# Turned blocks multiplied by the norm's weights once per PSUM bank, two low halves on GpSimd at two boundaries, and the orders around them laid anew

## The reference

```
def first_block(x, ...):            # mixer: RG-LRU branch + attention over 64 chosen keys
    h = rmsnorm(x, norm_mix_pre) @ w_in
    ...                             # rnn and attention, gated, then w_o
    x = x + rmsnorm(mix, norm_mix_post)
    h = rmsnorm(x, norm_ffn_pre)                 # boundary "f0"
    x = x + rmsnorm(swiglu(h), norm_ffn_post)
def second_block(x, ...):           # two layers
    for l in range(2):
        x = x + 0.5 * swiglu(rmsnorm(x, ffn1_norm[l]), ...)   # "f1", "f3"
        x = x + mixer_l(x)                                    # "ev" or "od"
        x = x + 0.5 * swiglu(rmsnorm(x, ffn2_norm[l]), ...)   # "f2", "f4"
```

## Time and profile before

| | us |
|---|---|
| median of 3 runs | 1407.73 (1406.33 to 1409.03) |
| profiled execution, own time | 1409.42 |
| its span | 1407.6 |
| PE busy | 1385.2 (98%) |
| DVE busy | 967.2 (69%) |
| ACT busy | 810.4 (58%) |
| POOL busy | 53.5 (4%) |

### The profile page before, as it was taken

The page is one execution under the profiler, slowest core; times in us unless marked ns, Lnnn a source line. Parts: engine busy times, 40 slices in busy tenths (PEclk is TensorE's granted clock), DMA queues, the critical chain, the costliest instruction groups (busy, mean ns, idle before and its releaser), DMA issues.

```text
span 1407.6 us, 19523 instructions
## 1 busy us (share of the span) xinstructions
PE 1385.2 (98%) x7290; PEld 1175.5 (84%) x7290; DVE 967.2 (69%) x1472; ACT 810.4 (58%) x1264; POOL 53.5 (4%) x62
## 2 busy tenths in 40 slices
PE   8999999999999999999999999999999999999999
PEld 7898788788887888888788888888888877888887
DVE  7999856667755676756977777556675584667753
ACT  6679944565645555545866555445554576565541
POOL 2021000000000000000000000000000070000000
PEclk9999999999999999999999999999999999999999
DMA  9544455476555566566346665566655541366651
GB/s 314 173 121 135 153 162 182 133 224 182 191 186 173 177 185 185 189 187 198 110 164 197 185 188 190 185 192 182 181 193 181 160 150 31 121 208 186 190 193 60
DMA packets 127213, 242.64 MB, mean 172 GB/s; under 512 B 7568, under 2 KB 13328, under 8 KB 127120
## 3 DMA queue, kind: packets, MB, share of 16 engines
q1 hardware_dynamic: 126208, 239.15, 55.0%
q0 software_dynamic: 624, 2.10, 0.5%
q10 hardware_dynamic: 288, 0.14, 0.0%
HBM read 240.31 MB, written 1.05 MB: 171 GB/s over the span
## 4 chain that ended last, share of the span: by engine, by line
PE 93%; DVE 4%; ACT 2%; issue 1%; DMA 0%; ACTq 0%; DVEq 0%
PE PX L347 24%; PE PX L361 16%; PE PX L363 16%; PE PX L362 16%; PE PX L349 12%; PE PX L407 3%; PE PX L652 2%; DVE WL L328 1%; PE PX L541 1%; PE PX L355 1%; PE PX L356 1%; PE PX L357 1%; PE PX L545 0%; ACT WH L322 0%; PE PX L1055 0%
## 5 line engine op out<-in xcount | busy, mean ns | idle before, releaser
L328 DVE TENSOR_TENSOR WL<-RAW,WH 128x1024 fp32r<-128x1024 f32 (+2 forms) x454 | 554.7, 1227 | 356.2 <-ACT WH L322 354.0
L322 ACT ACTIVATE WH<-RAW 128x1024 fp32r<-128x1024 f32 (+2 forms) x454 | 477.1, 1054 | 507.6 <-PE PX L363 268.1
L347 PE MATMUL PX<-AT,WH 128*128 128x512 f32 x1440 | 508.1, 398 | 0.0
L349 PE MATMUL PX<-AT,WL 128*128 128x256 f32 x1440 | 403.3, 280 | 0.0
L347 PEld LDWEIGHTS PX<-AT,WH 128*128 128x128 f32 x1440 | 270.5, 188 | 65.9
L349 PEld LDWEIGHTS PX<-AT,WL 128*128 128x128 f32 x1440 | 271.7, 189 | 0.2
L361 PE MATMUL PX<-WH,AT 128*128 128x512 f32 (+4 forms) x528 | 210.7, 399 | 6.4 <-DVE AT L1312 6.0
L363 PE MATMUL PX<-WH,AT 128*128 128x512 f32 (+4 forms) x528 | 201.9, 382 | 0.0
L362 PE MATMUL PX<-WL,AT 128*128 128x512 f32 (+4 forms) x528 | 201.4, 381 | 0.0
L361 PE MATMUL PX<-WH,FTh 128*128 128x512 f32 x440 | 171.6, 390 | 0.0
L363 PE MATMUL PX<-WH,FTl 128*128 128x512 f32 x440 | 171.3, 389 | 0.0
(11 more groups left out here) (333 smaller groups left out, 1327.9 us busy)
## 6 DMA issues: line engine op xcount, KB each, us to landing
RAW<-in_ffn_w_gu_dram SPq DMA_DIRECT2D x132, 512.0 KB, 3.7
RAW<-in_ffn_w_gu_2b_dram SPq DMA_DIRECT2D x88, 512.0 KB, 3.7
RAW<-in_w_in_dram SPq DMA_DIRECT2D x44, 512.0 KB, 3.7
RAW<-in_ffn_w_down_dram SPq DMA_DIRECT2D x44, 512.0 KB, 3.3
RAW<-in_ffn_w_down_2b_dram SPq DMA_DIRECT2D x44, 512.0 KB, 3.3
RAW<-in_w_ffn_down_dram SPq DMA_DIRECT2D x22, 512.0 KB, 3.6
RAW<-in_ev_w_in_dram SPq DMA_DIRECT2D x20, 512.0 KB, 3.6
RAW<-in_w_rnn_out_dram SPq DMA_DIRECT2D x8, 512.0 KB, 3.7
```

The source lines that it names most:

```text
L322: e.activation(WH[i % NHL][:, 0:m], RAW[i % NRAW][:, 0:m], ACT.Copy).then_inc(*up("hi", i))
L328: e.tensor_tensor(WL[i % NHL][:, 0:m], RAW[i % NRAW][:, 0:m], WH[i % NHL][:, 0:m].bitcast(F32), ALU.subtract).then_inc(*up("lo", i))
L347: e.matmul(PB[bank].rearrange("p (h s) -> p h s", h=2), h[:, f], AT0B[:, :, kx, :], start=start, stop=False, skip_group_check=True)
L349: ins = e.matmul(PB[bank][:, 0:S], l[:, f], p.src[0][:, kx, :], start=False, stop=stop, skip_group_check=True)
```

## The change

A new function `dve_block_gain` multiplies a whole bank by the norm's weights in one instruction, with the weights broadcast along the tokens, into a new SBUF tile XG; `act_block_hi` and `dve_block_lo` become one instruction each, from XG. At f0 and f1 the `lo` of the third and of the fourth chunk (chunks 76, 77 and 142, 143) runs on GpSimd, with a semaphore of its own, which `mm` and the loads into RAW wait for. The orders of PE, ACT, DVE and POOL in the start, the first mixer and at the four boundaries are laid anew. Nothing else is computed, and SP's order is the same.

```
+        POOL_LOW = [F[f][0][0].first + x for f in (0, 1) for x in (2, 3)]
...
+        def low(e, i):
+            m = stream[i][2] * stream[i][4]
+            e.wait_ge(*on("hi", i))
+            e.tensor_tensor(WL[i % NHL][:, 0:m], RAW[i % NRAW][:, 0:m], WH[i % NHL][:, 0:m].bitcast(F32),
+                            ALU.subtract).then_inc(*up(LOW(i), i))
...
+        def pool_lo(e, f, x):
+            low(e, F[f][0][0].first + x)
...
+        def dve_block_gain(e, n, b, c):
+
+            i = COLS[GAIN[n][0]] + GAIN[n][1] + 4 * c
+            e.wait_ge(*on("b_T", (n, b, c)))
+            e.tensor_tensor(block_room(b, c), PB[4 + 2 * b + c].rearrange("p (t s) -> p t s", t=4),
+                            CO[:, i:i + 4].unsqueeze(2).broadcast_to([128, 4, 128]), ALU.mult).then_inc(*up("b_g", (n, b, c)))
...
-            for i in range(4):
-                t = 4 * c + i
-                ins = e.activation(AT0[0][:, t, b * 128:b * 128 + 128], bank[:, i * 128:i * 128 + 128], ACT.Copy,
-                                   scale=gain(n, t))
-            ins.then_inc(*up("b_hi", (n, b, c)))
+            e.wait_ge(*on("b_g", (n, b, c)))
+            e.activation(AT0[0][:, 4 * c:4 * c + 4, b * 128:b * 128 + 128], block_room(b, c),
+                         ACT.Copy).then_inc(*up("b_hi", (n, b, c)))
...
+            e.tensor_tensor(AT0[1][:, 4 * c:4 * c + 4, b * 128:b * 128 + 128], block_room(b, c), hi_,
+                            ALU.subtract).then_inc(*up("b_lo", (n, b, c)))
```

More of the change, by code:

```diff
@@ L322, in hi, with LOW @@
                 e.activation(WH[i % NHL][:, 0:m], RAW[i % NRAW][:, 0:m], ACT.Copy).then_inc(*up("hi", i))
-        def lo(e, i):
[L325 to L329, removed]
+        POOL_LOW = [F[f][0][0].first + x for f in (0, 1) for x in (2, 3)]
+        def LOW(i):
+            return "lo_p" if i in POOL_LOW else "lo"
+        def low(e, i):
[3 more added lines that the diff above has]
+                            ALU.subtract).then_inc(*up(LOW(i), i))
+        def lo(e, i):
+            if i < len(stream) and i not in POOL_LOW:
+                low(e, i)
+        def pool_lo(e, f, x):
+            low(e, F[f][0][0].first + x)
         def mm(e, p, i, b):
@@ L2240, in pe_first_mixer @@
             pe_gates(e, 2)
+            dense(e, GR1, 2, 5)
+            pe_scores(e, AT_A, 3)
+            dense(e, GR1, 5, 9)
+            pe_turn_p(e, AT_A, 1)
+            dense(e, GR1, 9, 11)
+            pe_values(e, AT_A, 1)
+            pe_turn_q(e, AT_A, 1)
+            dense(e, GR1, 11, 16)
+            dense(e, GA0, 0, 1)
+            pe_gates(e, 3)
+            dense(e, GA0, 1, 4)
+            pe_scores(e, AT_A, 4)
+            pe_scores(e, AT_A, 5)
+            dense(e, GA0, 4, 5)
@@ L2241, in pe_first_mixer @@
+            pe_scores(e, AT_A, 6)
+            dense(e, GA0, 5, 8)
+            dense(e, GA1, 0, 5)
+            pe_turn_p(e, AT_A, 2)
+            dense(e, GA1, 5, 6)
+            pe_values(e, AT_A, 2)
+            pe_turn_p(e, AT_A, 3)
+            dense(e, GA1, 6, 7)
+            pe_values(e, AT_A, 3)
             pe_turn_p(e, AT_A, 4)
-            pe_values(e, AT_A, 3)
-            dense(e, GR1, 2, 5)
+            dense(e, GA1, 7, 8)
+            dense(e, GB0, 0, 1)
             pe_values(e, AT_A, 4)
-            dense(e, GR1, 5, 16)
@@ L2267, in pe_first_mixer @@
             pe_scores(e, AT_A, 11)
-            dense(e, GA1, 6, 8)
+            pe_turn_p(e, AT_A, 8)
+            dense(e, GB1, 0, 1)
+            pe_values(e, AT_A, 8)
             pe_turn_p(e, AT_A, 9)
-            pe_values(e, AT_A, 8)
-            dense(e, GB0, 0, 1)
+            dense(e, GB1, 1, 2)
+            pe_values(e, AT_A, 9)
             pe_turn_q(e, AT_A, 3)
-            pe_values(e, AT_A, 9)
-            dense(e, GB0, 1, 2)
+            dense(e, GB1, 2, 3)
             pe_scores(e, AT_A, 12)
+            pe_scores(e, AT_A, 13)
@@ L2564, in act_first_mixer @@
             hi(e, 24)
+            hi(e, 25)
+            hi(e, 26)
+            act_xr(e, 0, 0)
+            act_xr(e, 0, 1)
+            act_conv(e, 0, 0)
+            act_conv(e, 0, 1)
+            hi(e, 27)
+            act_conv(e, 1, 0)
+            act_conv(e, 1, 1)
+            hi(e, 28)
+            hi(e, 29)
             act_keys1(e, 0)
@@ L2630, in act_first_mixer @@
             act_ga(e, 0, 1)
-            hi(e, 41)
+            hi(e, 42)
+            hi(e, 43)
+            hi(e, 44)
+            act_exp(e, AT_A, 2)
+            hi(e, 45)
+            act_exp(e, AT_A, 3)
+            act_p(e, AT_A, 2)
+            act_exp(e, AT_A, 4)
+            hi(e, 46)
+            act_p(e, AT_A, 3)
+            act_gelu(e, 0, 1)
+            act_p(e, AT_A, 4)
+            act_ga(e, 1, 0)
+            act_ga(e, 1, 1)
+            act_y(e, 1)
+            hi(e, 47)
+            hi(e, 48)
@@ L3029, in dve_first_mixer @@
             dve_gx(e, 1)
+            lo(e, 31)
+            lo(e, 32)
+            lo(e, 33)
+            dve_conv(e, 3, 0)
+            lo(e, 34)
+            dve_conv(e, 3, 1)
+            dve_decay(e, 1)
+            lo(e, 35)
+            dve_max(e, AT_A, 1)
+            dve_input(e, 0)
+            lo(e, 36)
+            dve_scan(e, 0)
+            lo(e, 37)
+            dve_input(e, 1)
+            dve_gx(e, 2)
+            dve_decay(e, 2)
+            lo(e, 38)
+            dve_scan(e, 1)
@@ L3406, in pool_program @@
             pool_post(e, "f0")
+            pool_lo(e, 0, 2)
+            pool_lo(e, 0, 3)
             pool_post(e, "f1")
+            pool_lo(e, 1, 2)
+            pool_lo(e, 1, 3)
             pool_even(e)
```

509 lines of the change are left out of this document (228 added, 281 removed).

## The result

The changed kernel takes 1412.38 us in the median of 18 runs (1407.19 to 1415.45), the kernel before 1409.09 (1406.33 to 1410.38). The ratio is 1.0022, 95% interval [1.0015, 1.0029]: slower by about 3 us, just over the 0.2% named above. The time lies in the range that was given (1402.5 to 1414.5) and 2.6 us above the forecast of 1409.8. Of these 2.6 us 1.4 are the base: the forecast stood on a median of 3 runs of the kernel before (1407.73), and its median of 18 runs is 1409.09. The change itself was forecast at +2.0 us and measured at +3.1 (by the ratio).

The account below looks back on a forecast made before the run. PE, working in 98% of the span, was taken as the bound. Terms +1.15 + 0.4 - 0.8 + 1.25 + 0 = +2.0 us gave 1411.4 in the profiled execution, stated as 1409.8 for the median; range 1402.5 to 1414.5.

Parts of the forecast that it names:

- The hold: Everywhere: a DVE instruction with both operands in SBUF and a POOL instruction exclude each other; first come goes first.
- Rival 1: Faster: no hold for these instructions, so f0 and f1 gain, -5.3 us in all, 1402.4 us; chance 0.20.
- f0: Boundary f0: DVE goes first, PE's first pass starts at 265.4 instead of 266.16, -0.8 us.
- f1: Boundary f1: first pass +0.9 us if DVE is first, +1.6 if POOL; mean +1.25, bounds +0.3 and +2.4.
- rival 3: POOL is first at both boundaries: f0 +0.5, f1 +1.6, +1.65 us in all, 1411.5 us; chance 0.10.
- Clock: Behind f0 and f1: the low clock stays at both, since idle times near 3 us stay.
- The start: At the spread: PE arrives sooner and stands 1.7 instead of 0.53 us, +1.15; bounds 0 and +1.6.
- f2, f4: Boundaries f2 and f4: one PE pass fewer ahead of half 1's turns, no POOL; no term in the sum.
- The first mixer: First mixer: 48 instead of 44 switches between passes and other PE work, about 0.1 us each, +0.4 us.
- I take 0: First mixer: PE's stalls do not change, judged by summed DVE and ACT work; 0 us, bounds -1.2 and +4.
- a sign of being wrong: Mixer: DVE's order makes a `lo` late that the sums, knowing no waits between ACT and DVE, had in time.
- Rival 2: Slower: first mixer's tail stalls PE at attention's turns in units 8 to 15, +3.5 us, 1413.3 us; chance 0.22.

Follow-up runs that it names:

- mixer_only: The kernel before with only the changed orders of the start and the first mixer; 1411.39 us against 1409.35, ratio 1.0016.
- xr_wait: The changed kernel with one POOL multiplication, pool_xr(1, 0), also waiting for DVE's convolution (1, 1); 1411.01 us against 1408.65 of before, ratio 1.0021.
- bounds_only: The changed kernel with the start and the first mixer of the kernel before; 1408.72 us against 1409.35 of before, ratio 0.9994.
- old_block: Kernel before with its own block functions and mixer, PE's turns moved, POOL's low halves behind block (0,1)'s sum; ratio 0.9932, the second time 0.9945.
- pool_later: bounds_only with GpSimd's low halves at f0 and f1 also waiting for the sum of block (0,1); 1408.66 us, ratio 1.0000.

## Why the prediction came out as it did

- **The hold**: right. A 128x1024 subtraction on POOL takes 2.37 to 2.38 us unheld (I had 2.2, bounds 1.9 and 2.57; its rows of 2.80 to 2.95 include time in which it stood itself), and the two held instructions at f0 have the lengths of the walk (2.12 us against 2.15, 1.46 against 1.5). At f1 the held ones were post(0,0), 2.94, and the addition, 2.11, not `lo` 144, since POOL was first. Rival 1 is refuted.
- **f0**: -0.8 forecast, -0.78 measured, with DVE first. **f1**: POOL was first (rival 3, there alone): +1.6 forecast for that case, +1.53 measured; my term, a mean of both cases, was +1.25.
- **Clock**: I had it fall behind both as before. It fell at f0 and not at f1 in the profiled execution, and over all runs up to once less: 1.1 to 1.8 us that no term of mine had, in the kernel's favour.
- **The start**: +1.15 forecast; PE idles 1.07 us at the spread in after, 1.50 in mixer_only and 1.63 in xr_wait, against 0.53 in before and 0 to 0.89 in the eight other runs with its start: +1.0 in the mean. Late it is by 0.88 to 1.27 us in all, of which about 0.8 is the change's (above).
- **f2, f4**: 0 forecast, 0 measured (from 612 us to the odd mixer, and from there to the end, PE's lateness stays within 0.05 us).
- **The first mixer is the term that was mis-sized**: +0.4 forecast, +2.46 and +2.41 measured. The step that failed is "I take 0" for PE's stalls. Inside the mixer PE idles 3.6 us in after against 1.4 in before. I had summed each engine's work up to each chunk, without the hold and without waits between ACT and DVE. The new order put POOL's XR1 rows beside the convolution that gates(1) needs, by the very mechanism that I had read from the trace (0.9 us of the 2.46, by xr_wait). I had named such a miss as a sign of being wrong, but for a `lo`, not for a convolution. The rest (1.1 us at the scores and smaller waits) is not traced to one cause; a convolution held by POOL (three instructions in 3.46 us, 1.52 elsewhere) and the table load stand ahead of it on DVE and ACT, but no run separates them.
- **Rival 2** gave a near number (1413.3) for a wrong reason: the waits for attention's turns are 0.22 us at most and 0.4 in all, where it had +3.5 us.

Sum of the terms: 1.15 + 0.4 - 0.8 + 1.25 = 2.0 forecast; 1.27 + 2.46 - 0.77 + 1.53 = 4.5 in the trace, less 1.1 to 1.8 for the clock. That the change came out near its forecast is in part luck: of the mixer's miss of 2.1 us, 1.1 to 1.8 were offset by falls of the clock that did not come.

## What to carry to other kernels

- Before work goes to GpSimd, list the vector instructions with two SBUF operands that will run beside it: each is held for the rest of a GpSimd instruction (by up to 2.2 us here: 2.94 in place of 0.75). What reads PSUM is not, so keep such a form (before's block_lo) where the two overlap.
- Look first at the order on the engine that ends the wait. Moving four low halves behind the block that PE waits for, with PE's turns and ACT's copies moved to suit, was worth 7 us in the time (4.4 to 5.5 of them seen at the two boundaries), with GpSimd or without; the new instruction was worth nothing in the old orders and cost time in the new ones.
- Sums of work per engine show that there is room, not that nothing waits. Where an order is laid anew, walk the places with two engines and one deadline.

## What the runs showed of the hardware

- The hold applies to a 128x1 instruction too: 0.77 us and 1.75 us instead of 0.16. A DVE instruction with one SBUF operand was not held (one instance, in xr_wait L926, a 128x512 TENSOR_SCALAR, 0.43 us from 94.81, inside POOL's work from 93.48 to 96.37).
- The clock's fall behind a stall is not certain. After an idle time of 2.3 us in the odd mixer it fell in before and stayed in after; at f0, behind the same 2.4 us of idle time, it fell in after and stayed in bounds_only. Behind the 0.65 us stalls of old_block at f0 and f1 it did not fall in either profiled execution. Most falls to 1.2 GHz lasted 3.4 us, three lasted 6.8 (f1 in mixer_only and pool_later, the odd mixer in old_block).
- The same pairs of matmuls (128x512 and 128x256) ran at two paces with the clock at 1.00 throughout. Groups of PE in 510 to 575 us, first of before, then of after:

```profile
L347 PE MATMUL PX<-AT,WH 128*128 128x512 f32 x185 | 65.4, 399 | 0.0
L349 PE MATMUL PX<-AT,WL 128*128 128x256 f32 x184 | 51.7, 281 | 0.0
```

```profile
L360 PE MATMUL PX<-AT,WH 128*128 128x512 f32 x188 | 65.2, 394 | 0.0
L362 PE MATMUL PX<-AT,WL 128*128 128x256 f32 x189 | 52.4, 277 | 0.0
```

  185 pairs against 188 in the same 65 us. Before had the faster pace in F[4] only, after in F[1] too (1.6 us). This is why traces were compared part by part; what sets the pace is open. Single executions of one kernel differ by up to 8 us here, and much of that goes with the clock: of the changed kernel's 18 runs the two at a mean clock of 0.995 took 1414.3 and 1414.5 us, the one at 1.000 took 1407.2.
